# Moving weight splits and a softplus chain in a two-block transformer kernel on Trainium2

## The reference

```python
def _rglru_mixer(h, w_in, conv_w, conv_b, gate_a_w, gate_a_b, gate_x_w, gate_x_b, lam, w_out):
    gate, xr = jnp.split(h @ w_in, 2, axis=-1)          # 1024 -> 2 x 1280
    gate = jax.nn.gelu(gate)
    xr = _causal_dwconv(xr, conv_w) + conv_b            # 4 taps
    xh = xr.reshape(b, s, A_HEADS, A_HEAD_DIM)          # 16 heads of 80
    r = jax.nn.sigmoid(einsum("bshi,hij->bshj", xh, gate_a_w) + gate_a_b)
    ig = jax.nn.sigmoid(einsum("bshi,hij->bshj", xh, gate_x_w) + gate_x_b)
    log_a = -LRU_C * r * jax.nn.softplus(-lam)
    a = jnp.exp(log_a)
    u = jnp.sqrt(-jnp.expm1(2.0 * log_a)) * (ig * xr)
    _, hs = lax.associative_scan(_lru_combine, (a, u), axis=1)
    return (hs * gate) @ w_out
```

## Time and profile before

| | |
|---|---|
| median of 3 runs | 3505.44 us (3499.66 to 3510.98) |
| the profiled execution | 3499.66 us, its span 3497.9 us |
| busy: PE, PEld | 3381.7 us (97%), 2766.8 us (79%) |
| busy: DVE, ACT, POOL | 1753.9 us (50%), 1185.9 us (34%), 485.9 us (14%) |
| mean granted clock of TensorE | 0.989 of full |

### The profile page before, as it was taken

One profiled execution on the slowest core, in us unless ns is written; L12 is line 12 of the kernel. 1 busy time (PEld: TensorE's weight loads), 2 busy tenths in 40 slices (PEclk: granted clock), 3 DMA queues, 4 the chain that ended last, 5 costly groups with the idle time before them and its releaser, 6 DMA issues. The chain is left out here.

```text
span 3497.9 us, 51578 instructions
## 1 busy us (share of the span) xinstructions
PE 3381.7 (97%) x21476; PEld 2766.8 (79%) x21476; DVE 1753.9 (50%) x1938; ACT 1185.9 (34%) x1477; POOL 485.9 (14%) x435
## 2 busy tenths in 40 slices
PE   7999999999999999999999999999998888999998
PEld 6588888888888888887588888887777776878887
DVE  7665243364345554345665253655686444555242
ACT  3632122432222232222632124234664442332122
POOL 2111011021011021011111012000141120111011
PEclk9999999999999999999999999999999998999999
DMA  4233333223232233233233323333322114313322
GB/s 131 63 101 96 96 96 108 83 87 106 88 104 84 97 100 105 91 102 104 68 97 96 102 92 107 114 125 115 102 89 65 40 49 137 105 60 96 96 96 73
DMA packets 314085, 329.54 MB, mean 94 GB/s; under 512 B 22834, under 2 KB 305461, under 8 KB 313397
## 3 DMA queue, kind: packets, MB, share of 16 engines
q1 hardware_dynamic: 307141, 303.39, 27.2%
q0 software_dynamic: 4464, 19.40, 1.7%
q10 hardware_dynamic: 2304, 4.20, 0.3%
HBM read 312.28 MB, written 14.68 MB: 93 GB/s over the span
## 5 line engine op out<-in xcount | busy, mean ns | idle before, releaser
L488 PE MATMUL ps<-xh,wh 128*128 128x512 f32 x2360 | 930.5, 394 | 10.1 <-DVE wl L425 10.1
L488 PE MATMUL ps<-xh,wl 128*128 128x512 f32 x2360 | 919.9, 390 | 0.0
L488 PE MATMUL ps<-xl,wh 128*128 128x512 f32 x2360 | 919.7, 390 | 0.0
L425 DVE TENSOR_TENSOR wl<-raw,wh 128x2048 fp32r<-128x2048 f32 (+2 forms) x286 | 639.9, 2237 | 425.5 <-ACT wh L420 424.8
L420 ACT ACTIVATE wh<-raw 128x2048 fp32r<-128x2048 f32 (+2 forms) x287 | 527.5, 1838 | 712.3 <-PE ps L488 677.0
L488 PEld LDWEIGHTS ps<-xh,wh 128*128 128x128 f32 x2360 | 444.0, 188 | 114.9 <-issue 23.6
L488 PEld LDWEIGHTS ps<-xl,wh 128*128 128x128 f32 x2360 | 444.1, 188 | 95.5 <-issue 4.3
L488 PEld LDWEIGHTS ps<-xh,wl 128*128 128x128 f32 x2360 | 443.7, 188 | 93.1
L488 PE MATMUL ps<-hh,wh 128*128 128x512 f32 x1280 | 498.5, 389 | 1.2 <-DVE wl L425 1.2
L488 PE MATMUL ps<-hl,wh 128*128 128x512 f32 x1280 | 498.0, 389 | 0.0
L488 PE MATMUL ps<-hh,wl 128*128 128x512 f32 x1280 | 498.0, 389 | 0.0
(11 more groups left out here) (420 smaller groups left out, 3590.1 us busy)
## 6 DMA issues: line engine op xcount, KB each, us to landing
raw<-in_mlp_w SPq DMA_DIRECT2D x128, 1024.0 KB, 5.3
raw<-in_ffn_w SPq DMA_DIRECT2D x32, 1024.0 KB, 5.3
raw<-in_w_in SPq DMA_DIRECT2D x31, 1024.0 KB, 5.4
raw<-in_a_w_in SPq DMA_DIRECT2D x20, 1024.0 KB, 5.0
raw<-in_c_w_in SPq DMA_DIRECT2D x12, 1024.0 KB, 5.1
raw<-in_a_w_out SPq DMA_DIRECT2D x16, 640.0 KB, 4.1
raw<-in_b_w_in SPq DMA_DIRECT2D x8, 1024.0 KB, 5.3
raw<-in_xa_wkv SPq DMA_DIRECT2D x8, 1024.0 KB, 6.1
```

Of the source, the lines that this page charges most:

```text
L425: nc.vector.tensor_tensor(wl[:, p.slot(su), 0:n], raw[:, p.slot(su), 0:n], wh[:, p.slot(su), 0:n], ALU.subtract).then_inc(lower, 1)
L488: last = nc.tensor.matmul(banks[mt][:, 0:st.n], wt[at_, slot, k, mt * P:mt * P + P], ops[oi][at_, kk, 0:st.n], start=k == 0 and su == 0 an ...
```

## The change

Four things move, and nothing is added to or taken from the computation.

1. The `wl` of the very first unit is formed by DVE, ahead of everything else in its list, instead of by POOL.
2. The softplus of lambda is done in one piece at the start: DVE's 27 chained operations follow |lambda| directly, and ACT's Sqrt and Exp of small vectors follow at the end of `act_init`. `act_branch` and `dve_softplus_end` as separate functions go.
3. The two special places for splits go: gate's unit 1 is split at the head of gate's group 0, and out's unit 1 at the head of out's group 0 (as `split_next` does for all others).
4. In branch, the second bank is brought out of PSUM after the convolution of the first tile instead of before it.

```diff
@@ split_next
-            if p.c == 0 and (st.kind == "agate" or st.kb == 5 and su == 0):
-                continue
             fn(eng, p, su + 1)
@@ pool_init
-        pool_split(pool, At(order[0], 0, 0, 0))
@@ dve_init
         dve_lower(dve, stages["init"], G_MIX, ND - 1)
-        dve.wait_ge(lower, 3)
@@ act_init
         act_resplit(act, stages["init"], G_MIX, 0)
-    def act_branch(p):
-        if p.c != 3:
-            return
-        act = nc.scalar
         act.wait_ge(s("lambda_abs"), 1)
         act.wait_ge(s("prm_ready"), 5)
         act.activation(prm[1][:, G_SQ:G_SQ + ND], prm[1][:, G_SQ:G_SQ + ND], ACT.Sqrt)
...
@@ dve_softplus
         nc.vector.tensor_copy(lab, lab).then_inc(s("lambda_abs"), 1)
-    def dve_softplus_end(dve):
         dve.wait_ge(s("lambda_exp"), 1)
         link(nc.vector.tensor_scalar(z, e, 2.0, None, ALU.add))
...
@@ dve_conv4
-            for mt in range(2):
-                nc.vector.tensor_tensor(xpad[:, mt, 3:3 + T], ps[b + mt][:], rs[:], ALU.mult).then_inc(evac, 1)
             for mt in range(2):
...
+                nc.vector.tensor_tensor(xpad[:, mt, 3:3 + T], ps[b + mt][:], rs[:], ALU.mult).then_inc(evac, 1)
                 nc.vector.wait_ge(evac, p.group() * 2 + 5 + mt)
@@ act_a, after tiles 4 and 5
-            if t0 == 4:
-                act_split(act, At(stages[n + "_gate"], 0, 0, 0), 1)
@@ dve_a
-        if l == 0:
-            dve_softplus_end(dve)
...
-            if t == 5:
-                dve_split(dve, At(stages[n + "_gate"], 0, 0, 0), 1)
@@ act_gate, group 4
-                act_split(nc.scalar, p, 2)
@@ dve_gate, group 4
-            if j == 4:
-                dve_split(nc.vector, p, 2)
@@ the lists of ACT and DVE
-                act_stage(act, G[f"l{l}_branch"], custom=act_branch if l == 0 else None)
+                act_stage(act, G[f"l{l}_branch"])
...
+        dve_split(dve, At(order[0], 0, 0, 0), 0)
         dve_init(dve)
         dve_softplus(dve)
```

More of the change, by code:

```diff
@@ L728, in pool_init @@
         pool.wait_ge(made, 8)
-        pool_split(pool, At(order[0], 0, 0, 0))
         pool_squares(pool, stages["init"])
-    def pool_split(pool, p):
-        pool.wait_ge(upper, p.unit(0) + 1)
-        nc.gpsimd.tensor_tensor(wl[:, p.slot(0)], raw[:, p.slot(0)], wh[:, p.slot(0)], ALU.subtract).then_inc(lower, 1)
     def pool_squares(pool, norm):
@@ L809, in dve_softplus @@
         lam = prm[2][:, LAM:LAM + 20]
-        lab, z = small[:, 4:24], small[:, 44:64]
+        lab, e, z, z2, q = (small[:, 4:24], small[:, 24:44], small[:, 44:64], c8[:, 0], c8[:, 1])
         link(nc.vector.tensor_scalar(z, lam, -1.0, None, ALU.mult))
@@ L813, in dve_softplus @@
         nc.vector.tensor_copy(lab, lab).then_inc(s("lambda_abs"), 1)
-    def dve_softplus_end(dve):
-        lam = prm[2][:, LAM:LAM + 20]
-        e, z, z2, q = (small[:, 24:44], small[:, 44:64], c8[:, 0], c8[:, 1])
         dve.wait_ge(s("lambda_exp"), 1)
```

## The result

| | before | changed |
|---|---|---|
| median | 3505.19 us (6 runs) | 3525.40 us (3518.82 to 3527.53, 6 runs) |
| ratio | | 1.0055, 95% interval 1.0044 to 1.0066 |
| profiled span | 3497.9 us | 3523.6 us |

The changed kernel is 20.2 us slower by the medians. The sum of the prediction was +20.5. Five more executions of it, the profiled one among them, took 3521.34 to 3529.60 us.

A forecast was written before the change was run, and what follows sets the result against it. PE, busy for 97% of the span, was taken as the bound. Layer 0's +8.9 and layer 3's +11.55 gave +20.5 us; on the median of 3505.44 the forecast was 3526 us, range 3513 to 3539.

The forecast's parts named there:

- the four waits: PE waiting for wl of unit 1 in layers 0 and 3: 5.3 us in each gate, 3.9 us in each out.
- Part 1: At the start, the first wl on DVE: first xl takes 0.7 to 1.2 us, DVE late by 0.6 to 1.1 us.
- Part 2: Softplus at the start: PE stands still some 6.3 us before group 1, unit 2 ready at 60.7, shift +6.4 us.
- the bound of 61.5: Latest time for branch's group 2 in layer 0 if PE's clock falls, against 60.7 expected.
- The gain of 8.8 us in pe_a: Layer 0, chain gone from the head of dve_a: pe_a's 49.94 us becomes layer 3's 41.11; contained in gate's -5.4 us.
- Part 3: Gate: PE idles 5.3 us, -5.4 us in layer 0, +3.4 in layer 3; out: +3.9 us in each layer.
- Part 4: Branch's order: 0.25 us a group, showing only before group 2; already counted in layer 0, +0.25 us in layer 3.
- The clock: Half clock after new stalls: 2.4 us for each gate, 1.6 for each out, bounds 0 and 3.2; hidden at the start.
- The clock holds: Rival: no half-clock loss after the four later stalls in gate and out; +12.5 us, 3518, chance 0.14.
- The start is covered: Rival: PE need not wait before group 1, so 6.4 us go; +6.1 us with full clock, 3511.5, chance 0.04.
- Part 3 does nothing: Rival: unit 1's splits in time in gate and out; -2.4 us, less up to 3.8, 3499 to 3503, chance 0.03.
- Everything is exposed: Rival: Sqrt load, start's clock, 3.2 us after all four stalls, clock loss in layer 0's pe_a; +30.6 us, 3536, chance 0.14.

The follow-up runs named there:

- experiment 11: Kernel before with only the first unit's wl formed on DVE, first in its list; one execution, 3497.53 us.
- Experiment 9: Changed kernel with the softplus chain behind wl of unit 1 and the norm's reciprocal instead of ahead of them; 3532.50 us, 1.0074.
- experiment 1: Kernel before with only the first wl on DVE and the softplus in one piece at the start; 3504.17 us, 1.0005.
- experiment 5: Kernel before with the 27 chained operations moved from the head of dve_a to branch's group 4 in layer 0; 3496.77 us, 0.9979.
- experiment 2: Kernel before with only gate's unit 1 split at the head of gate's group 0; 3517.97 us, 1.0034.
- experiment 3: Kernel before with only out's unit 1 split at the head of out's group 0; 3522.59 us, 1.0042.
- experiment 10: Kernel before with only branch's second bank brought out after the first tile's convolution; 3507.04 us, 1.0006.
- experiment 4: Changed kernel (the filled kernel) with 20 unused matmuls in each gate's stall and 14 in each out's; 3515.43 us, 1.0028.

## Why the prediction was right

The prediction held: 3526 was forecast, 3525.4 measured, and the four waits behind it are where they were forecast. That the two numbers are 0.6 us apart is luck, since the interval of the change is +15 to +23 us, and since the sum was worked out against one profile in which unchanged code reached pe_a at 87.28, where it reached it at 90.2 in others. Point by point, with the changed kernel's profile:

| step | forecast | profile |
|---|---|---|
| first xl ends | 23.5 to 24.0 | 23.4 |
| wl of unit 1 | 47.4 | 46.97 |
| PE's wait before group 1 | 6.3 | 4.9 |
| wl of unit 2 | 60.7 | 60.15 |
| pe_a of layer 0 begins later by | 6.4 | 6.31 (93.59) |
| wait in gate | 5.3 | 5.13, 5.13 |
| wait in out | 3.9 | 3.77, 3.76 |
| half clock after gate's, after out's (layer 0), against the filled kernel | 2.4, 1.6 | 3.0, 1.5 |
| the same in layer 3 | 2.4, 1.6 | 2.7, 1.4 |
| layer 0 in all | 8.9 | 9.5 |
| layer 3 in all | 11.55 | 12.2 |

*Part 1* cost nothing: experiment 11 shows it, through the 0.75 us xl that the prediction reckoned with.

*Part 2.* The wait before group 1 was 1.4 us too long in the forecast, because PE's sum for the norm began at 41.19, not at some 40.1 (its first group ran longer at half clock, with matmuls of 0.63 us until 32.1, before until 28.9), and because `wl` came 0.4 earlier. It hardly mattered, since unit 2 is ready at 60.15 however long that wait is. The forecast had the half clock of the start hidden behind DVE. It was so with the start alone and with the stalls filled, where PE starts group 2 at 60.17 and 60.34, right after unit 2. In the changed kernel's own profile group 1 took 2.8 us longer than at full clock and PE came to group 2 at 60.86, so 0.7 us of it was not hidden, within the bound of 61.5. Experiment 9 shows the weight of unit 2: it removed most of the first wait, made unit 2 later, and the kernel was slower. The gain of 8.8 us in pe_a is shown twice, in experiments 1 and 5. ACT's table load for Sqrt was hidden, as assumed, and no drain shows after a load: Exp's row starts at 38.34, when the load that began at 37.04 has taken its 1.28. Of the price that the Trainium skill (ScalarE: Activation LUTs, "What ACT_TABLE_LOAD costs") gives for a switch, the load's 1.28 us is seen here, and the drain of about 1.4 us is not.

*Part 3* is where the slowdown is: two waits of 5.13 and two of 3.8 us, each shown alone in experiments 2 and 3. In the kernel before, both splits were done when PE asked for these weights. Gate's cost pe_a 1.8 us where it stood (41.11 us in layer 3, against 39.31 without it), which the forecast counts as given back; out's cost PE nothing there.

*Part 4* is +0.26 a layer, experiment 10.

*The clock* was the least certain term and a little too small. By the stretches of experiment 4 the four stalls lose 8.6 us together, where the sum had 8.0: the gate stalls' 2.4 was low (3.0 and 2.7), the out stalls' 1.6 was right. That is half of the difference between 20.5 and the 21.7 us of the mark at 2192. The rest is in tenths: gate's group 1 is 0.2 us later than worked out in each layer, and branch of layer 3 takes 0.4 us more, not 0.25. The prediction also read a 3.0 us stall in layer 0 as one that costs nothing; it cost nothing in that profile and 1.6 us in others. The medians' +20.2 against the mark's +21.7 is within the interval of the ratio (+15 to +23).

*The rivals.* "The clock holds" would have been +12.5; experiment 4, in which it holds at the four stalls, ended at +10.2 by the medians. "The start is covered" was impossible in this order of the lists, yet its mechanism exists: experiment 5 covers the chain and is 8.7 us faster than before. "Part 3 does nothing" is experiment 1, which has no part 3: no change, as that rival said of its time. "Everything is exposed" is out: Sqrt's load was hidden, no stall cost more than 3.2 us of clock, and pe_a of layer 0 took 39.3 us.

## What to carry to other kernels

Where one engine is busy for 97% of the span, ask of every piece of work on another engine which later piece stands behind it in its list, and when the busy engine asks for that one; the first stall that appears need not be the one that sets the time (experiment 9). Work of a few us costs 8.8, some 3 to 6, or 0 us by where it stands, and the place that costs nothing is in the timeline: an idle time of its engine while the next weights are already there. A stall also costs what the clock does after it, here two fifths to three fifths more on top of the wait, so two short splits in the wrong place (in each of two layers) were worth more than a chain of 27 operations.

## What was not expected

The same kernel, profiled twice, differed by 12.4 us in one stretch of 834 us and by 0.3 us in the 2192 us before it. Over the same 9928 instructions PE was busy 13.4 us longer, at a granted clock of 0.96 instead of 0.98. Anyone who compares two single profiles by their spans would read this as an effect of an edit; marks at the same instruction in both show where it is not, and stretches that begin and end around the edit repeat within 0.2 us.

The same wait of 3.00 us before branch's group 2 was followed by no half clock in some executions and by 1.6 us of loss in others.

Matmuls whose result nobody reads made a kernel 10 us faster: with them, the granted clock behind stalls of 3.8 and 5.1 us stayed at full (2.4 GHz).
